# A decoder layer on one core: the last attention round's gate passes laid over slots 9 to 23, and the loads of finished outputs moved three slots later

## The chip, the cores and the metric

The kernel is one program on one core of a Trainium2 chip. Its time is device microseconds (us) of one execution, and the median over runs counts. The engines run side by side and meet at semaphores: TensorE (PE) multiplies, VectorE (DVE), ScalarE (ACT) and GpSimd (POOL) work elementwise, SyncE (SP) issues weight transfers, and ACT's queue issues all other transfers.

## What is computed

One layer of a decoder over 1024 tokens of width 1024, in float32, cut here to what matters:

```
n = rmsnorm(h); proj = n @ w_in         # q, k, v of mixers A and B, gates A and B
o_a = dilated_attention(qa, ka, va)     # 8 heads of 64, softmax under three patterns
o_b = stick_breaking(qb, kb, vb)        # 8 heads of 64, strictly causal
mixed = sigmoid(gate_a) * (o_a @ w_up_a) + sigmoid(gate_b) * (o_b @ w_up_b)
h = h + mixed @ w_out
h = h + memory_attention(rmsnorm(h), rmsnorm(mem))
h = h + swiglu(rmsnorm(h))
return rmsnorm(h)
```

## The kernel before

Everything lies transposed, features on the 128 partitions and the 1024 tokens along the row, in 8 tiles. Precision is kept by splitting each operand into a high and a low part. A product of a weight tile with the 8 operand tiles is therefore three **passes** (high by high, high by low, low by high) of 8 matmuls of 512 columns for each half of the tokens, six passes for a tile. POOL splits each weight tile (`w_hi`, `w_lo`), two buffers deep.

Attention runs in four rounds, one pair of heads of A and one of B each. Three rounds use the plan `ROUND` in a loop, the fourth uses `LAST`, written out. A round is 28 **slots**. There are 24 chunks of up to 512 keys, A's in slots 0 to 11, B's in slots 12 to 23. In slot s PE does, in this order: `logits(s)` (L496), `attend(s - 4)` (L533), `transposes(s - 3)` (L510), and then the **fill** of that slot, passes of the projection tiles (L387). The fill keeps PE at work while the other engines handle a chunk: ACT scales and takes exponentials, DVE runs the cumulative sums of B (`remaining`, L1307 and L1310), and the transposed weights are split into `pt` by ACT (L910) and DVE (L1340), on which `attend` of the next slot waits. DVE reads a finished half of a tile out of its bank (`read_out`, L1217) at the start of the slot behind the one that ended it. ACT stores a gate tile (L942) two slots behind its end.

`LAST` has seven tiles: KB, QB, VB, which feed B, and G0 to G3, gate tiles that nothing in the round reads. Slots 24 to 27 have no logits; they drain the pipeline. `attend(23)`, in slot 27, ends PE's work of the round.

Finished attention outputs go to memory (`store_o`, L965) and come back as the operand of the gated products. `LOAD_O` says in which slots ACT issues the loads of operand tiles 0 to 6 (L952), two in a slot, beginning two slots behind the last fill slot. `ROUND_O` says in which slots ACT already makes the high part of a loaded tile (`round_o`, L958), one in a slot; DVE makes the low part a slot later (`o_rest`, L1260). Tile 7 can be loaded only when the last store has landed (L987, L988). ACT then issues the first four loads of gates (L981), and rounds the tiles that `ROUND_O` left out. The gated product of a weight tile has four units of 12 matmuls each: two with operand tiles 0 to 3, which wait for four low parts, and two with tiles 4 to 7, which wait for all eight. After that PE works without a pause until the output projection.

Of the kernel before, what the change touches and what calls it, by code (L numbers as in the profile page):

```python
# [90 lines left out]
class Plan:  # L91
# [8 lines left out]
    def __init__(self, names, passes, transposes):  # L100
# [40 lines left out]
        for work in self.after["dve"]:  # L141
# [4 lines left out]
ROUND = Plan(("KB", "QB", "QA", "KA", "VB", "VA", "G0", "G1", "G2", "G3"),  # L146
             [3] * 6 + [2] * 6 + [3, 2, 3, 2, 3, 2, 2, 3, 2] + [1] * 6 + [2], {"TB": (12, 14), "TA": (18, 20)})
LAST = Plan(("KB", "QB", "VB", "G0", "G1", "G2", "G3"),
            [2] * 21 + [0] * 7, {"TB": (10, 12)})

LOAD_O = {max(LAST.end.values()) + 2 + n: [k for k in (2 * n, 2 * n + 1) if k < KT - 1] for n in range(4)}
ROUND_O = {min(LOAD_O) + 3 + k: k for k in range(4)}

RAW = {"QA": 0, "KA": 1, "VA": 2, "KB": 0, "QB": 1, "VB": 2, "G0": 0, "G1": 1, "G2": 0, "G3": 1}
SPLIT_NUMBER = {"KB": 3, "QB": 4, "QA": 5, "KA": 6, "TB": 3, "TA": 5}
# [8 lines left out]
def build(nc, xT, memT, positions, gains, weights, ident_d, rope_d, bias_d, mask_d, outT):  # L166
    with ExitStack() as ctx:
# [596 lines left out]
        def _(act):  # L764
# [96 lines left out]
            def round_(i, plan):  # L861
# [41 lines left out]
                for s in range(SLOTS + 2):  # L903
# [43 lines left out]
                    if plan is LAST and s in LOAD_O:  # L947
# [3 lines left out]
                        for k in LOAD_O[s]:  # L951
                            act.dma_start(n_lo[:, k, :].bitcast(F32), o_d[k]).then_inc(tile_in[k], 16)  # L952
                    if plan is LAST and s in ROUND_O:
                        round_o(ROUND_O[s])

            def round_o(k):
                act.wait_ge(tile_in[k], 32)
                act.activation(n_hi[:, k, :], n_lo[:, k, :].bitcast(F32), ACT.Copy).then_inc(o_hi_s, 1)  # L958
# [20 lines left out]
            def load_gates(j, b):  # L979
                for g, at in ((g_a, 0), (g_b, KT)):  # L980
                    act.dma_start(g[:, b, :], gates_d[bass.ds(j + at, 1), :, :].rearrange("o p n -> p (o n)")  # L981
                                  ).then_inc(g_in[b], 16)
# [7 lines left out]
            load_gates(1, 1)  # L990
            for k in range(len(ROUND_O), KT):
                round_o(k)
# [127 lines left out]
        def _(dve):  # L1120
# [99 lines left out]
            def lo_part(name, number, filled):  # L1220
                dst, hi = qk[name[1]][1 if name[0] == "Q" else 3], qk[name[1]][0 if name[0] == "Q" else 2]
                dve.wait_ge(bank_free, filled)
                dve.wait_ge(qk_hi_s, number)
                dve.tensor_tensor(dst[:], raw[:, RAW[name], :], hi[:].bitcast(F32), ALU.subtract).then_inc(qk_lo_s, 1)
# [32 lines left out]
            def o_rest(k):  # L1257

                dve.wait_ge(o_hi_s, k + 1)
                dve.tensor_tensor(n_lo[:, k, :], n_lo[:, k, :].bitcast(F32), n_hi[:, k, :].bitcast(F32),  # L1260
                                  ALU.subtract).then_inc(o_lo_s, 1)

            def round_(i, plan, links):
# [57 lines left out]
                for s in range(SLOTS + 2):  # L1321
# [35 lines left out]
                    for what, name, *rest in plan.after["dve"][s]:  # L1357
# [3 lines left out]
                        elif what == "lo":  # L1361
                            lo_part(name, i * 4 + SPLIT_NUMBER[name], bank + (unit + 2))
                    if plan is LAST and s - 1 in ROUND_O:
                        o_rest(ROUND_O[s - 1])
                assert local[0] == links
# [8 lines left out]

            for k in range(SLOTS + 1 - min(ROUND_O), KT):
                o_rest(k)
# [268 lines left out]
```

## Time and profile before

| what | value |
|---|---|
| median of 3 runs | 1899.01 us (1897.57 to 1899.85) |
| profiled execution, its own time | 1899.36 us |
| its span, first to last instruction | 1897.6 us |
| PE busy | 1782.4 us, 94% |
| DVE busy | 994.6 us, 52% |
| ACT busy | 629.1 us, 33% |
| POOL busy | 709.6 us, 37% |
| mean granted TensorE clock | 0.975 |

The profiled execution's own time is 1.8 us above its span; this lies before the first and after the last instruction. Times in rows are us from the span's start. The round `LAST` lies from 652.5 (its first logits) to 811.2 (end of its last `attend`), and the gated products begin at 817.2. A clock of 1.00 is the higher of TensorE's two levels, 0.50 the lower.

### The profile page before, as it was taken

What the parts mean: (1) busy time and instruction counts of PE and PEld (TensorE: products, weight loads), DVE (VectorE), ACT (ScalarE), POOL (GpSimd) and SP (SyncE); (2) the same over time, 40 slices, a digit from 0 to 9 for tenths busy, and PEclk for the clock granted to TensorE, in tenths of its full rate; (3) what the DMA queues carried; (4) which work ended last, traced back from release to release, by engine and by line L of the source; (5) the groups of instructions that cost most, each with busy time, mean ns of one, the idle gap of its engine ahead of it and who ended that gap; (6) DMA issues with size and microseconds to landing.
All of it is one profiled execution on the core that took longest, in us unless ns stands there. A gap on an engine that the chain in (4) does not pass through costs nothing.

```text
span 1897.6 us, 24569 instructions
## 1 busy us (share of the span) xinstructions
PE 1782.4 (94%) x8610; PEld 1446.1 (76%) x8610; DVE 994.6 (52%) x1490; ACT 629.1 (33%) x1009; POOL 709.6 (37%) x848
## 2 busy tenths in 40 slices
PE   3799999999999999789999899999999999999996
PEld 3677777777778777668887777888888888888884
DVE  7446894688469757865434553332332333333236
ACT  4215773576367557743113332000000000000003
POOL 5632223132313122134553034444434434443435
PEclk8899999999999999889999999999999999999998
DMA  5311112112111211263212011111111111111112
GB/s 191 123 46 46 31 51 64 46 39 66 49 46 38 77 40 50 90 221 133 78 55 78 12 34 45 52 48 44 44 55 44 45 55 44 44 49 50 44 44 89
DMA packets 42201, 118.59 MB, mean 62 GB/s; under 512 B 5136, under 2 KB 13584, under 8 KB 42000
## 3 DMA queue, kind: packets, MB, share of 16 engines
q1 hardware_dynamic: 21312, 75.66, 11.8%
q10 hardware_dynamic: 20816, 41.95, 6.7%
q8 instruction: 46, 0.75, 0.2%
q14 instruction: 27, 0.22, 0.0%
HBM read 97.67 MB, written 18.87 MB: 61 GB/s over the span
## 4 chain that ended last, share of the span: by engine, by line
PE 83%; DVE 7%; ACT 3%; issue 3%; DVEq 0%; ACTq 0%; POOL 0%; DMA 0%; POOLq 0%
PE ps L387 70%; PE ps L533 4%; PE ps L496 3%; PE ps L510 3%; DVE e_row L1310 1%; DVE e_row L1307 1%; DVE pt L1340 1%; DVE h L1550 1%; DVE rows L1319 1%; ACT n_hi L1028 1%; PE ps L529 1%; DVE rms L1421 1%; DVE h L1410 0%; ACT p_m L1054 0%; PE ps L663 0%
## 5 line engine op out<-in xcount | busy, mean ns | idle before, releaser
L350 POOL TENSOR_SCALAR w_hi<-w_stage 128x512 fp32r<-128x512 f32 x276 | 200.9, 745 | 1159.3 <-issue 622.5
L355 POOL TENSOR_TENSOR w_lo<-w_stage,w_hi 128x256 fp32r<-128x256 f32 x552 | 487.4, 913 | 11.5
L387 PE MATMUL ps<-n_hi,w_hi 128*128 128x512 f32 x1536 | 395.2, 398 | 11.0 <-DVE n_lo L1260 7.0
L387 PE MATMUL ps<-n_lo,w_hi 128*128 128x512 f32 x1536 | 386.2, 392 | 0.0
L387 PE MATMUL ps<-n_hi,w_lo 128*128 128x512 f32 x1536 | 385.7, 391 | 0.0
L387 PEld LDWEIGHTS ps<-n_hi,w_hi 128*128 128x128 f32 x1536 | 288.1, 190 | 74.0 <-issue 12.0
L387 PEld LDWEIGHTS ps<-n_lo,w_hi 128*128 128x128 f32 x1536 | 287.3, 188 | 59.8 <-issue 0.2
L387 PEld LDWEIGHTS ps<-n_hi,w_lo 128*128 128x128 f32 x1536 | 286.0, 188 | 58.6
L1410 DVE TENSOR_TENSOR h<-ps,h 128x512 f32<-128x512 f32 (+1 forms) x192 | 132.1, 691 | 160.0 <-PE ps L387 160.0
L1083 ACT ACTIVATE a_hi<-u_f 128x1024 fp32r<-128x1024 f32 x22 | 23.4, 1065 | 466.3 <-DVE u_f L1516 466.3
L1508 DVE TENSOR_TENSOR u_f<-ps,rms 128x512 f32<-128x512 f32 x44 | 30.4, 692 | 205.3 <-PE ps L387 205.3
L910 ACT ACTIVATE pt<-ps 128x256 fp32r<-128x256 f32 (+3 forms) x96 | 77.9, 811 | 134.0 <-PE ps L510 133.9
L1340 DVE TENSOR_TENSOR pt<-ps,pt 128x256 fp32r<-128x256 f32 (+3 forms) x96 | 91.9, 957 | 49.7 <-ACT pt L910 45.6
L387 PE MATMUL ps<-a_hi,w_hi 128*128 128x512 f32 x352 | 111.3, 395 | 1.7 <-DVE a_lo L1518 1.7
L387 PE MATMUL ps<-a_hi,w_lo 128*128 128x512 f32 x352 | 111.7, 396 | 0.0
L387 PE MATMUL ps<-a_lo,w_hi 128*128 128x512 f32 x352 | 111.5, 396 | 0.0
L1217 DVE TENSOR_TENSOR raw<-ps,rms 128x512 f32<-128x512 f32 x80 | 54.8, 685 | 92.5 <-PE ps L387 92.5
L1508 DVE TENSOR_TENSOR g_f<-ps,rms 128x512 f32<-128x512 f32 x44 | 30.3, 691 | 123.1 <-PE ps L387 120.9
L1081 ACT ACTIVATE g_f<-g_f 128x1024 f32<-128x1024 f32 x22 | 23.3, 1061 | 177.8 <-DVE g_f L1508 177.7
L510 PE MATMUL ps<-ident,rows 128*128 128x128 f32 x576 | 81.4, 279 | 0.0
L387 PEld LDWEIGHTS ps<-a_hi,w_hi 128*128 128x128 f32 x352 | 66.1, 188 | 18.8 <-DVE a_lo L1518 2.1
L387 PEld LDWEIGHTS ps<-a_hi,w_lo 128*128 128x128 f32 x352 | 66.1, 188 | 16.2
(175 smaller groups left out, 2212.2 us busy)
## 6 DMA issues: line engine op xcount, KB each, us to landing
w_stage<-weights_in SPq DMA_DIRECT2D x138, 512.0 KB, 3.3
gates_scratch<-raw ACTq DMA_DIRECT2D x16, 512.0 KB, 2.8
o_scratch<-o_sum ACTq DMA_DIRECT2D x64, 64.0 KB, 2.1
n_lo<-o_scratch ACTq DMA_DIRECT2D x8, 512.0 KB, 3.8
g_a<-gates_scratch ACTq DMA_DIRECT2D x8, 512.0 KB, 3.7
g_b<-gates_scratch ACTq DMA_DIRECT2D x8, 512.0 KB, 4.5
h<-x_t_in ACTq DMA_DIRECT2D x8, 512.0 KB, 7.5
out_t<-h ACTq DMA_DIRECT2D x16, 256.0 KB, 2.1
```

Of the source, the lines that this page charges most:

```text
L350: ins = pool.tensor_scalar(w_hi[:, b, at], stage[:, b, at], 1.0, 1.0, ALU.mult, ALU.mult)
L355: ins = pool.tensor_tensor(w_lo[:, b, at], stage[:, b, at], w_hi[:, b, at].bitcast(F32), ALU.subtract)
L387: ins = pe.matmul(bank, w[:, b, c:c + P], mv(k), start=(first and n == 0), stop=(last and n == total - 1))
L496: ins = pe.matmul(ps[:, 2 + h, 0:width(s)], a[hs, blk(qb)], b[hs, at], start=(n == 0), stop=(n == 2 and not diagonal))
L510: ins = pe.transpose(ps_t[:, h, n, :], rows[:, s % 4, h, blk(n)], ident[:])
L533: ins = pe.matmul(ps[:, r, blk(h, 2 * P)], v_of[m][:, c + kb, h, :, :].rearrange("p a d -> p (a d)"), pt[:, h, kb, :, :].rearrange("p a q ...
L910: act.activation(pt[:, :, 0:n, 0, :], ps_t[:, :, 0:n, :], ACT.Copy).then_inc(pt_hi_s, 1)
L1083: act.activation(a_hi[:, f, :], u_f[:, f, :], ACT.Copy).then_inc(a_hi_s, 1)
L1217: dve.tensor_tensor(raw[:, RAW[name], blk(half, HALF)], ps[:, half, :], rms[:, blk(half, HALF)], ALU.mult).then_inc(bank_free, 1)
L1340: dve.tensor_tensor(pt[:, :, 0:n, 1, :], ps_t[:, :, 0:n, :], pt[:, :, 0:n, 0, :].bitcast(F32), ALU.subtract).then_inc(pt_lo_s, 1)
L1410: dve.tensor_tensor(hj, ps[:, bank + half, :], hj, ALU.add).then_inc(bank_free, 1)
L1508: dve.tensor_tensor(dst[:, blk(half, HALF)], ps[:, bank + half, :], rms[:, blk(half, HALF)], ALU.mult).then_inc(bank_free, 1)
```

## The change

Two of the plan's lists change. The 18 passes of KB, QB and VB in slots 0 to 8 stay as they are. The 24 gate passes lay two to a slot in slots 9 to 20; now slots 10, 13, 15, 18, 20 and 22 have one and slots 9, 11, 12, 14, 16, 17, 19, 21 and 23 have two. Since the last fill slot is 23 and no longer 20, `LOAD_O` begins in slot 25 and no longer in slot 22 (25, 26, 27 with two loads, 28 with one). `ROUND_O` is cut to two entries, in slots 28 and 29, where it had four, in slots 25 to 28. The tiles 2 and 3 thus join the tiles 4 to 7 behind the round.

```
 LAST = Plan(("KB", "QB", "VB", "G0", "G1", "G2", "G3"),
-            [2] * 21 + [0] * 7, {"TB": (10, 12)})
+            [2] * 9 + [2, 1, 2, 2, 1, 2, 1, 2, 2, 1, 2, 1, 2, 1, 2] + [0] * 4, {"TB": (10, 12)})
...
 LOAD_O = {max(LAST.end.values()) + 2 + n: [k for k in (2 * n, 2 * n + 1) if k < KT - 1] for n in range(4)}
-ROUND_O = {min(LOAD_O) + 3 + k: k for k in range(4)}
+ROUND_O = {min(LOAD_O) + 3 + k: k for k in range(2)}
```

The reads and stores follow the passes. Reads of gate halves were in slots 11, 12, 14, 15, 17, 18, 20 and 21, and are now in slots 11, 13, 15, 17, 18, 20, 22 and 24. Stores were in slots 13, 16, 19 and 22, and are now in slots 14, 18, 21 and 25.

## Rows read from the trace of the kernel before

**Rows 1.** Busy time and granted clock, by stretch of the round's end.

```profile
core 0: us, PE busy (x) PEld busy (x) DVE busy (x) ACT busy (x) POOL busy (x), PEclk, DMA share, GB/s
...
731.30:792.50 61.20, 53.11 (x318) 42.42 (x316) 58.80 (x68) 50.27 (x64) 13.14 (x12) 1.00 0.15 49
792.50:811.20 18.70, 10.65 (x48) 9.21 (x48) 11.95 (x22) 9.87 (x19) 0.00 (x0) 0.61 0.68 236
811.20:825.80 14.60, 7.59 (x27) 5.60 (x26) 12.06 (x12) 10.07 (x11) 7.58 (x6) 0.68 0.69 244
```

**Rows 2.** Timeline of PE, slot 10's fill and the logits behind it.

```profile
710.56 1.98 PE L387 MATMUL ps<-n_hi,w_hi 128*128 128x512 f32 x8
712.47 0.96 PE L496 MATMUL ps<-qk 64*128 64x512 f32 x6
```

**Rows 3.** Timeline of ACT, slots 11 and 12.

```profile
716.79 0.72 ACT L873 ACTIVATE rows<-rows,stat 128x512 f32<-128x512 f32 x1 [0.30 <-DVE stat L1291]
...
720.19 1.02 ACT L887 ACTIVATE rows<-ps 128x1024 f32<-128x1024 f32 x1 [0.46 <-PE ps L500]
722.07 1.02 ACT L910 ACTIVATE pt<-ps 128x1024 fp32r<-128x1024 f32 x1 [0.85 <-PE ps L510]
```

**Rows 4.** Timeline of DVE, its stretch without pauses and the two pauses in it.

```profile
731.34 1.23 DVE L1307 SCALAR_TENSOR_TENSOR e_row<-rows,e_row 128x1024 f32<-128x1024 f32 x1 [2.44 <-ACT e_row L897]
...
738.24 0.68 DVE L1217 TENSOR_TENSOR raw<-ps,rms 128x512 f32<-128x512 f32 x1
...
764.92 1.23 DVE L1307 SCALAR_TENSOR_TENSOR e_row<-rows,e_row 128x1024 f32<-128x1024 f32 x1 [0.72 <-ACT e_row L897]
...
777.19 1.23 DVE L1307 SCALAR_TENSOR_TENSOR e_row<-rows,e_row 128x1024 f32<-128x1024 f32 x1 [0.65 <-ACT e_row L897]
```

**Rows 5.** Timeline of ACT, slot 22: the step that takes `logits(22)`.

```profile
788.84 0.60 ACT L887 ACTIVATE rows<-ps 128x512 f32<-128x512 f32 x1
```

**Rows 6.** Timeline of PE: a slot's attend and transposes at the higher clock.

```profile
743.86 1.22 PE L533 MATMUL ps<-pt,vA 128*128 128x256 f32 x8 [0.50 <-DVE pt L1340]
744.92 1.03 PE L510 MATMUL ps<-ident,rows 128*128 128x128 f32 x8
```

**Rows 7.** Timeline of PE, slots 23 to 27 and the first gated products.

```profile
793.80 2.07 PE L533 MATMUL ps<-pt,vB 128*128 128x256 f32 x8 [3.39 <-DVE pt L1340]
795.67 1.91 PE L510 MATMUL ps<-ident,rows 128*128 128x128 f32 x8
800.02 2.08 PE L533 MATMUL ps<-pt,vB 128*128 128x256 f32 x8 [2.44 <-DVE pt L1340]
801.90 1.48 PE L510 MATMUL ps<-ident,rows 128*128 128x128 f32 x6
...
808.17 1.22 PE L533 MATMUL ps<-pt,vB 128*128 128x256 f32 x4 [1.41 <-DVE pt L1340]
...
810.75 0.79 PE L533 MATMUL ps<-pt,vB 128*128 128x256 f32 x2 [0.93 <-DVE pt L1340]
817.20 2.07 PE L387 MATMUL ps<-n_hi,w_hi 128*128 128x512 f32 x4 [5.65 <-DVE n_lo L1260]
...
825.77 1.19 PE L387 MATMUL ps<-n_hi,w_hi 128*128 128x512 f32 x4 [1.36 <-DVE n_lo L1260]
```

**Rows 8.** Chain that ended last, from the last store to the last low part.

```profile
813.49 2.10 DMA o_scratch<-o_sum
...
818.28 1.06 ACT n_hi L958
819.37 2.90 DVE n_lo L1260 x2
```

**Rows 9.** ACT's queue: one slot's issues of transfers.

```profile
793.14 0.64 ACTq L965 DMA_DIRECT2D o_scratch<-o_sum  x1
793.90 1.03 ACTq L952 DMA_DIRECT2D n_lo<-o_scratch  x2
```

**Rows 10.** Granted clock around the first gated products (columns as in rows 1).

```profile
820.00:821.00 1.00, 1.00 (x5) 0.81 (x4) 1.00 (x2) 1.00 (x2) 1.00 (x1) 0.80 0.81 315
```

## The prediction

> **What bounds the kernel now.** I read the page first: PE is busy for 94% of the span, so a change of order pays only where PE stands idle or runs at the lower clock. Next came the windows over the last attention round. From 731.3 to 792.5 it has 8.1 us of idle time in 61.2, and DVE is busy for 58.8 of these [rows 1]: DVE paces slots 13 to 22. From 792.5 to 811.2 PE works 10.65 of 18.7 us, at a mean clock of 0.61, and no engine is near full [rows 1]: each slot of the drain is a chain attend, transposes, ACT `pt`, DVE `pt`. From 811.2 to 825.8 PE waits for the operand tiles of the gated products. From 825.77 on, where all eight low parts are there, PE has no idle time to the output projection at 997. So the whole change is worth what it does to the start of the third gated unit, now at 825.77 [rows 7]. That start is my measure. I call the start of `attend(23)` Z, and the end of DVE's `pt` step before it differs from it by 0.04 us. Z is at 810.75, and the third unit starts at Z + 15.0.
>
> **Part 1, five passes taken out of slots 10 to 20.** A pass costs 1.9 us: the second of slot 10 begins at 710.56 and the logits behind it at 712.47 [rows 2]. Slot 10 has one fewer, and PE has no pause there, so `logits(11)` and `logits(12)` come 1.9 us sooner. The other engines do not follow in full. ACT's exponentials of slot 11 wait for DVE's maxima at 716.79 [rows 3], which stand behind DVE's and ACT's own work of slot 10, not behind PE. They fill ACT up to 719.7. The `scaled(12)` step waited 0.46 us for PE and can gain only that. Behind it, `pt` of slot 12 waited 0.85 us more for the transposes, so it moves by at most 0.46 + 0.85 = 1.3 us, and with small gaps I take 1.4. The softmax normalisation, the three softplus steps and with them DVE's first `remaining` (731.34, after 2.44 us of idle time [rows 4]) follow by these **-1.4**. The bounds are 0 and -1.9.
>
> From there DVE paces. Slots 13, 15, 18 and 20 have one pass fewer, but PE's passes there are hidden behind DVE, which has only two pauses, 0.72 and 0.65 us [rows 4]. The first ends with softplus(17), whose logits stand behind slot 16, which keeps two passes; it stays. The second stands behind slots 17 and 18, of which 18 loses a pass: it gives about **-0.35** until DVE's own work is the limit. Bounds 0 and -1.4.
>
> What DVE itself has to do changes by one read. In slots 14 to 22 there were six reads of gate halves and are now five. The one of slot 14 (738.24, 0.6 us from start to start of the next) goes to slot 13, into the pause of 2.44 us before `remaining` [rows 4]: **-0.6**. The one of slot 21 goes to slot 22, and that cancels. The last one goes to slot 24, where DVE waits for the transposes anyway. So `attend(19)`, now at 793.80, moves by -1.4 - 0.35 - 0.6 = -2.35, to 791.45.
>
> **Part 2, five passes added in slots 21 to 23.** In slot 21 two passes (3.8 us) come behind the transposes. They fill the time in which PE waited for `attend(18)` and delay `logits(22)`, but ACT took these logits only at 788.84, right behind its own work [rows 5], so nothing waits. Slot 22's pass lies in the 3.39 us before `attend(19)` [rows 7]. In slot 23 the two passes stand between `transposes(20)` and `attend(20)`. PE waited 2.44 us there. The passes take 3.7, so 1.3 us is not covered.
>
> They also change the clock. Now the clock has fallen by `attend(19)`, since PE did little in slots 22 and 23 before it. `attend(19)` and `transposes(20)` take 3.8 us, where the same pair at the higher clock takes 1.9 [rows 6]. With PE at work through slots 21 to 23 I take the higher clock up to `transposes(21)`. Then from `attend(19)` to `attend(20)` it is 1.9 + 3.75 = 5.65 where it was 6.22: **-0.57**. `attend(20)` and `transposes(21)` take 1.8 for 3.37: **-1.56**. Of the rest, some at the lower clock now (1.22 us for the four matmuls at 808.17 [rows 7]), I take **-0.3**; bounds +1.0 and -0.6, since slots 25 to 27 stay sparse. Sum: Z moves by -2.35 - 0.57 - 1.56 - 0.3 = **-4.8**, to 805.95. At the lower clock throughout, the second part is worth about 0 and Z moves by -2.4.
>
> **Part 3, loads and roundings later.** ACT's queue needs 0.64 us for a store and 1.03 for two loads [rows 9]. In slot 25 these and the gate store are 2.0 us between two `pt` steps that lie some 2.5 apart, so they are just covered. In slot 27 they lie between `o_low(23)` and the last store. Now that store goes out at 813.49 [rows 8], Z + 2.75, held up by a low part that DVE makes before `o_sum(23)`. After the change it follows the loads of slot 27, at Z + 2.6. No difference. It lands after 2.1 us, and the load of tile 7 and four loads of gates take 2.6 us more on the queue. At Z + 7.4 ACT can round again, as now (Z + 7.5, 818.28 [rows 8]). But now it begins with tile 4, and will begin with tile 2. PE's start needs tiles 2 and 3: two roundings of 1.0, and a low part of 1.2, so it comes at Z + 7.4 + 2.0 + 1.2 = Z + 10.6 instead of Z + 6.45. The two units before the third, at the lower clock first, took 7.2 us. The third unit then starts at Z + 17.8, not Z + 15.0: **+2.8**. If the units ran at the higher clock, the last low part would decide, at about Z + 16.9: **+1.9**. Above, the stretch at the lower clock could be twice as long: it ended 3.2 us behind PE's start [rows 7, 10]; under the sparse work of slots 23 and 24 it held from 793.8 to 803.4 [rows 7]. A second such stretch costs 1.7 us more: **+4.5**. I take +2.8.
>
> **Sum.** -4.8 + 2.8 = -2.0 us. The profiled execution took 1899.36, 0.35 above the median of the runs, and 1.8 of it lies outside its span. Neither changes, so the forecast is 1899.0 - 2.0 = **1897.0 us**. The bounds of the terms: with -6.0 for Z and +1.9 it is -4.1; with -2.4 and +4.5 it is +2.1.
>
> **Other work that moves.** POOL's splits of tiles G3 and of the first gated weight move from 746 and 766 to about 753 and 777, still inside DVE's stretch: the same number of collisions. DVE's reads of gates find their banks full, the closest in slot 20 by about 0.1 us by my slot sums. The gates, loaded at the same distance behind Z, are needed only when four units are done.
>
> **Rivals.** *Clock and roundings take it back* (slower). PE is idle for 10 us before the gated products, not 5.65, and the drain is sparse. If the clock falls again before `attend(20)`, Z gains only 2.9 us (the -2.35 and the -0.57), and if the two first gated units run low for longer, +2.8 + 1.7 = 4.5 stands against it: +1.6, 1900.6 us. It decides when the clock is low for more than 5 us behind PE's start. For it: the clock now falls twice between 792 and 811 and is at 0.5 at 817. Against: the passes fill exactly the time in which it fell. The Trainium skill ("TensorE: Matmul & The Clock Gate", section "What's actually happening") says that the low clock is the default and that only activity releases it. The rows agree for the falls seen; the rule speaks for this rival at the gated products, and against it in slots 22 to 24. By it alone the result would lie between this rival and the forecast.
>
> *PE paces more than I think* (faster). If DVE's stretch shrinks by both pauses and slot 10's pass counts in full, `attend(19)` moves by -1.9 - 1.4 - 0.6 = -3.9 and Z by -6.3, and the third unit by -3.5 to -4.4: about 1895.1 us. For it: PE is busy for 53.1 us of the same 61.2 and decides when softplus can begin in the slots behind the pauses. Against: DVE was busy for 96% of the stretch [rows 1, 4].
>
> *Nothing moves* (no change): the start of the chain in slot 12 is held by ACT after all, -1.4 falls away, and the drain gains just what the two roundings cost: -0.6 to +0.4, about 1899 us.
>
> **Chances.** Forecast 0.45, nothing moves 0.23, faster rival 0.15, slower rival 0.17. 0.2% is 3.8 us, and this is about what a measurement of this kernel can tell from no change. Only the faster rival reaches past it, in about half of its cases, and the slower one needs more than its price. Faster 0.11, same 0.82, slower 0.07. The range takes the faster rival's centre and most of the slower one's: 1894.8 to 1900.6.
>
> **What would show it.** In the trace of the changed kernel: DVE's first `remaining` some 1.4 us earlier; `attend(19)` at about 791.5; clock 1.00 up to 798; Z at about 806; PE's first gated product 10.6 us behind Z, the third unit 17.8 behind it. The forecast is wrong if the clock is low in slot 24, if DVE has new pauses between 729 and 790, if the queue's issues in slots 25 to 27 stretch the drain, or if something behind 825.8, which I took as moved in one piece, does not move with it.

## The result, and the profile after

The changed kernel takes 1906.85 us (median of 6, 1902.65 to 1909.55) where before takes 1899.03 (median of 6). The ratio is 1.0039, with a 95% interval of 1.0026 to 1.0052: slower, by 7.8 us by the medians and by about 7.4 by the ratio. Forecast were 1897.0 and a range up to 1900.6. The profiled execution took 1906.71, its span is 1904.9.

The timeline of PE in the changed kernel, around slot 14 (behind slot 13, which lost a pass) and in slot 19:

```profile
730.39 0.80 PE L496 MATMUL ps<-qk 64*128 64x384 f32 x6 [1.28 <-ACT rows L887]
...
734.62 0.77 PE L529 MATMUL ps<-pt,zero_r 128*128 128x512 f32 x1 [3.07 <-issue]
735.18 1.91 PE L533 MATMUL ps<-pt,vA 128*128 128x256 f32 x8
736.89 1.91 PE L510 MATMUL ps<-ident,rows 128*128 128x128 f32 x8
738.45 2.31 PE L387 MATMUL ps<-n_hi,w_lo 128*128 128x512 f32 x8
...
769.04 1.59 PE L533 MATMUL ps<-pt,vB 128*128 128x256 f32 x8 [1.60 <-DVE pt L1340]
...
771.14 2.98 PE L387 MATMUL ps<-n_lo,w_hi 128*128 128x512 f32 x8
```

The eight transposes take 1.91 us, not the 1.03 of [rows 6]; a pass takes 2.98, not 1.9. The clock fell here. In the kernel before it did not, though PE stood for 2.69 us in one pause of slot 14:

```profile
736.51 0.47 PE L529 MATMUL ps<-pt,zero_r 128*128 128x512 f32 x1 [2.69 <-issue]
...
737.77 1.04 PE L510 MATMUL ps<-ident,rows 128*128 128x128 f32 x8
```

PE of the changed kernel at the end of the round:

```profile
795.23 1.22 PE L533 MATMUL ps<-pt,vB 128*128 128x256 f32 x8 [2.17 <-DVE pt L1340]
796.29 1.04 PE L510 MATMUL ps<-ident,rows 128*128 128x128 f32 x8
...
800.84 1.12 PE L533 MATMUL ps<-pt,vB 128*128 128x256 f32 x8
801.79 0.82 PE L510 MATMUL ps<-ident,rows 128*128 128x128 f32 x6
804.57 0.98 PE L533 MATMUL ps<-pt,vB 128*128 128x256 f32 x6 [1.96 <-DVE pt L1340]
...
809.99 0.80 PE L533 MATMUL ps<-pt,vB 128*128 128x256 f32 x2 [0.93 <-DVE pt L1340]
825.19 2.07 PE L387 MATMUL ps<-n_hi,w_hi 128*128 128x512 f32 x4 [14.41 <-DVE n_lo L1260]
```

These answer to [rows 7]. `attend(19)` comes at 795.23, later by 1.4 us and not earlier by 2.35. Z is at 809.99 (810.75 before). PE then stands idle for 14.41 us where it stood for 5.65. The third gated unit starts at 833.52, 7.75 behind the 825.77 of before, and this is the whole difference of the spans (7.3), give or take 0.5.

What fills the 15 us behind Z is shown by the chain that ended last:

```profile
806.42 2.66 DMA o_scratch<-o_sum
809.08 0.01 issue
809.09 0.01 ACT pt L910
809.10 3.97 DMA o_scratch<-o_sum
...
813.16 0.42 DVE o_sum L1353
813.59 0.02 issue
813.61 3.31 DMA o_scratch<-o_sum
816.92 2.00 issue
818.92 0.33 ACTq L988
```

Before, one landing of a store stood in this chain, the last, with 2.10 us [rows 8]. Now there are three, with 2.66, 3.97 and 3.31. The 2.00 us behind the last, in which the chain names nothing, belong to this store too. The 3.31 us end where ACT's roundings of tiles 0 and 1 end (816.92), and not where the store lands. The view of L965 in the window 813.6:813.7 gives the store's own landing, 5.2 us from its issue:

```profile
L965 ACTq DMA_DIRECT2D o_scratch<-o_sum x1: 617/617/617, 813.6 to 813.6; - x1
DMA to landing us min/median/max: 5.2/5.2/5.2
```

That is 818.8, and tile 7's load follows at 818.92. For the last store of before the same view has 2.1. `o_sum` for the last chunk waits too, for the store that empties its buffer. The stretches of the changed kernel (the columns of [rows 1]):

```profile
729.45:795.18 65.73, 55.45 (x311) 44.66 (x311) 59.78 (x69) 51.16 (x65) 15.56 (x12) 0.92 0.14 47
...
810.00:825.20 15.20, 0.79 (x3) 0.50 (x3) 6.64 (x9) 6.18 (x7) 0.00 (x0) 0.50 0.93 348
825.20:833.50 8.30, 8.30 (x24) 6.65 (x25) 5.72 (x5) 5.29 (x6) 6.70 (x6) 0.65 1.01 405
```

The last column but one says that the DMA engines were busy for 93% of the wait, moving 348 GB/s. From DVE's first `remaining` to the end of its step for `attend(19)` there are 65.73 us; DVE works for 59.78 of them. The same stretch of before:

```profile
731.34:793.75 62.41, 53.07 (x318) 42.38 (x316) 60.03 (x70) 51.08 (x64) 13.14 (x12) 0.99 0.15 49
```

DVE's idle time in it grew from 2.4 to 5.95 us.

### The profile page after: what moved, and what is told of

It is laid out like the page before. It is cut to its first block, busy times and chain, and to the rows that moved or that the text cites. A ratio compares the mean times of both kernels' runs of the same rounds, so it can differ in the third digit from the quotient of the medians.

```text
span 1904.9 us, 24569 instructions
## 1 busy us (share of the span) xinstructions
PE 1782.1 (94%) x8610; PEld 1446.0 (76%) x8610; DVE 994.1 (52%) x1490; ACT 628.6 (33%) x1009; POOL 712.2 (37%) x848
## 4 chain that ended last, share of the span: by engine, by line
PE 81%; DVE 7%; ACT 4%; issue 3%; DMA 1%; DVEq 0%; ACTq 0%; POOL 0%; POOLq 0%
PE ps L387 70%; PE ps L533 3%; PE ps L496 3%; PE ps L510 3%; DVE e_row L1310 1%; DVE e_row L1307 1%; DVE h L1550 1%; DVE pt L1340 1%; DVE rows L1319 1%; ACT n_hi L1028 1%; DMA o_scratch<-o_sum 1%; PE ps L529 1%; DVE rms L1421 1%; DVE h L1410 0%; ACT p_m L1054 0%
## 5 line engine op out<-in xcount | busy, mean ns | idle before, releaser
L387 PE MATMUL ps<-n_hi,w_hi 128*128 128x512 f32 x1536 | 395.4, 398 | 18.5 <-DVE n_lo L1260 14.4
L496 PE MATMUL ps<-qk 64*128 64x512 f32 (+3 forms) x576 | 77.8, 376 | 1.3 <-ACT rows L887 1.3
```

The lines of the kernel that those rows point to most:

```text
L387: ins = pe.matmul(bank, w[:, b, c:c + P], mv(k), start=(first and n == 0), stop=(last and n == total - 1))
L496: ins = pe.matmul(ps[:, 2 + h, 0:width(s)], a[hs, blk(qb)], b[hs, at], start=(n == 0), stop=(n == 2 and not diagonal))
```

## The experiments

Each ran beside the kernel before on one chip; e1 to e4 shared a chip, so did e5 to e8 and e9 to e12. The medians of before were 1898.53, 1899.40 and 1898.77, and a difference across these groups is taken between the distances to them. The profiled executions differ by up to 5 us before the round begins, so positions are compared as distances from the round's first logits (652.55 before, 652.59 after). "Third unit" is the start of the third gated unit. The table's positions are those of one profiled execution each; that of e8 took 1891.20, 4.9 below its median, the others lie within 2.3 of theirs.

| run | ratio to before (95%) | attend(19) | Z | store issued to tile 7's load | third unit |
|---|---|---|---|---|---|
| before | 1 | 141.25 | 158.20 | 2.16 | 173.22 |
| after | 1.0039 (1.0026 to 1.0052) | 142.64 | 157.40 | 5.31 | 180.93 |
| e1, loads late | 1.0033 (1.0020 to 1.0045) | 141.23 | 158.15 | 5.56 | 180.60 |
| e2, one slot earlier | 1.0030 (1.0021 to 1.0040) | 142.50 | 159.30 | 4.02 | 180.88 |
| e3, two loads behind store | 1.0032 (1.0020 to 1.0045) | 142.29 | 157.03 | 2.74 | 177.64 |
| e4, other spread | 1.0043 (1.0026 to 1.0059) | 142.84 | 157.83 | 5.91 | 181.02 |
| e5, after, small loads | 1.0006 (0.9997 to 1.0015) | 142.37 | 159.19 | 2.19 | 177.82 |
| e6, before, small loads | 0.9995 (0.9986 to 1.0004) | 141.28 | 158.24 | 2.16 | 173.08 |
| e7, loads late, small | 1.0016 (1.0007 to 1.0025) | 141.23 | 158.17 | 2.19 | 177.16 |
| e8, before, clock kept | 0.9983 (0.9974 to 0.9992) | 141.27 | 156.09 | 2.17 | 170.80 |
| e9, after, clock kept | 1.0022 (1.0012 to 1.0033) | 140.41 | 155.15 | 5.71 | 178.23 |
| e10, as e8, more | 0.9982 (0.9973 to 0.9990) | 141.21 | 154.33 | 2.17 | 169.06 |
| e11, one pass moved | 0.9971 (0.9960 to 0.9982) | 140.06 | 153.55 | 2.17 | 169.70 |
| e12, two roundings | 1.0021 (1.0013 to 1.0030) | 141.28 | 158.60 | 2.17 | 177.65 |

**e1, the loads alone.**

```
 # passes of before
-LOAD_O = {max(LAST.end.values()) + 2 + n: ...
-ROUND_O = {min(LOAD_O) + 3 + k: k for k in range(4)}
+LOAD_O = {max(LAST.end.values()) + 5 + n: ...
+ROUND_O = {min(LOAD_O) + 3 + k: k for k in range(2)}
```

> The passes of before with the later loads and the two roundings of after. Theory L (small stores of attention outputs land late because the 512 KB loads of slots 25 to 28 are in flight with them): the drain's attends stand where they stood before (the last at 810.8), the stores of its last slots take 3 to 5 us to land instead of 2.1, the first gated product starts some 15 us behind the last attend (6.5 before), and the time is 7 to 9 us above before. Rival R (only the two roundings that moved behind the last landing cost, and the rest of the loss comes from the moved passes): 3 to 4 us above before, stores landing in 2.1 us.

Measured: 6.2 us above before (1904.69 against 1898.53), Z where it was, the first product 14.5 us behind it, the third unit 7.4 later. The time lies between the two expectations, and its interval (3.8 to 8.5 us) touches both. Nearly the whole loss is here without any moved pass. In the chain of this run:

```profile
808.49 2.51 DMA o_scratch<-o_sum
...
812.13 3.31 DMA o_scratch<-o_sum
815.44 2.25 issue
817.69 0.33 ACTq L988
```

The view of L965 gives the last three stores 2.7, 4.1 and 5.5 us to their landing (the chain again shows 3.31 of the last). By these landings theory L holds, and rival R, which had them at 2.1, falls.

**e2, loads one slot earlier, three roundings.**

```
 # passes of after
+LOAD_O = {max(LAST.end.values()) + 1 + n: ...
+ROUND_O = {min(LOAD_O) + 3 + k: k for k in range(3)}
```

> The passes of after, loads beginning in slot 24 (one behind the last fill) instead of 25, three roundings in slots 27 to 29. Theory L: the last two stores meet fewer loads and one rounding less stands behind the last landing; the first gated product starts 10 to 12 us behind the last attend (15.2 in after), 3 to 5 us faster than after. Rival R: one rounding, 1 us faster than after.

Measured: the first product 13.55 behind Z, between the two expectations, and a ratio whose interval overlaps that of after. A store landed after 4.91 us, two ahead of the last; the last took 3.9. The loads had met other stores. Its Z is late for another reason: the clock fell in slot 23 (a pass took 3.32 us at 797.93), and from `attend(19)` to Z it is 16.8 us, not the 14.76 of after. This run tells the theories apart only by the landings.

**e3, two loads behind the last store.**

```
 # passes of after
-LOAD_O = {max(LAST.end.values()) + 2 + n: ...
+LOAD_O = {25: [0, 1], 26: [2, 3], 28: [4, 5, 6]}
```

> As after, but tiles 4 and 5 are loaded in slot 28, behind the issue of the last store, instead of in slot 27 ahead of it; roundings as in after. Theory L: the last store lands in about 2.1 to 2.7 us instead of 3.3 to 5.3, and the first gated product starts 2 to 3 us sooner behind the last attend than in after; 2 to 3 us faster than after. Rival R: no change against after.

Measured: in its chain the last store takes 2.67 us, and the first product starts 12.76 us behind Z, 2.4 sooner than in after. That is theory L's number. The times (1904.00; the interval overlaps that of after) can't tell 2.4 us apart from none. In its queue the last two stores are shown as one group:

```profile
811.14 2.89 ACTq L965 DMA_DIRECT2D o_scratch<-o_sum  x2
814.15 1.50 ACTq L952 DMA_DIRECT2D n_lo<-o_scratch  x3
...
816.17 0.33 ACTq L988 DMA_DIRECT2D n_lo<-o_scratch  x1
```

**e5 to e7, the loads' bytes taken away.** One edit, made to after, to before, and to e1. It is on the seven loads of L952; tile 7's load keeps its bytes, though the expectation speaks of eight:

```
-act.dma_start(n_lo[:, k, :].bitcast(F32), o_d[k]).then_inc(tile_in[k], 16)
+act.dma_start(n_lo[:, k, 0:16].bitcast(F32), o_d[k][:, 0:16]).then_inc(tile_in[k], 16)
```

> The kernel after, but the eight loads of finished outputs bring only 16 of 1024 columns each (the operand tiles then hold old values in the rest), so that they hardly use the DMA engines; issues, waits and roundings stay. Theory L (stores queue behind the loads' bytes): stores land in 2.1 us in slots 25 to 28, the first gated product starts 10 to 12 us behind the last attend instead of 15, and the time falls 3 to 5 us below after, to 2 to 4 us above before. Rival Q (the number of issues on ScalarE's queue costs, not their bytes): as after, 7 us above before.

> The kernel before with the same cut of its eight loads to 16 columns; the control for the two others. Theory L: its stores already landed in 2.1 us where they decided, so it gains at most 1 us. If it gains 3 us or more, the loads' bytes also cost before, and the theory explains less of the difference.

> The passes of before with the later loads and two roundings of after, loads cut to 16 columns. Set against e6 it is the price of two roundings and the later issues alone: the forecast's +2.8 (bounds +1.9 and +4.5). Set against e5 it is the price of the moved passes alone: the forecast said -4.8; from the profiles seen so far I now expect -1, between -2 and 0.

Measured: 1900.93, 1898.11 and 1902.48 us. Without the bytes after is 2.8 us above its control, e6, and with them it was 7.8 above before. The first product of e5 comes 11.04 us behind Z, as theory L had it. The control itself gains nothing that can be told. e7's ACT queue issues as many loads at the same places as e1's, and the store is followed by tile 7's load 2.19 us after its issue:

```profile
814.48 0.62 ACTq L965 DMA_DIRECT2D o_scratch<-o_sum  x1
815.21 0.53 ACTq L952 DMA_DIRECT2D n_lo<-o_scratch  x1
...
816.67 0.33 ACTq L988 DMA_DIRECT2D n_lo<-o_scratch  x1
```

So it is the bytes and not the issues; rival Q falls. The DMA engines' share of busy time behind the last attends shows the same. First the window 811 to 814 of e1, then two windows of e7, whose round lies 2.3 us later:

```profile
811.00:814.00 3.00, 0.00 (x0) 0.00 (x0) 0.53 (x2) 0.56 (x1) 0.00 (x0) 0.50 1.03 351
```

```profile
811.00:814.00 3.00, 0.79 (x2) 0.50 (x2) 2.06 (x5) 0.98 (x3) 0.00 (x0) 0.50 0.18 29
814.00:817.00 3.00, 0.00 (x0) 0.00 (x0) 0.12 (x1) 1.21 (x2) 0.00 (x0) 0.50 0.31 50
```

e7 against e6 is the price of two roundings moved behind the landing, with the bytes gone: 4.4 us by the medians, 4.1 by the third unit. e5 against e7 is the price of the moved passes: -1.6 us by the medians, +0.7 in the two profiles. The profile of e5 is one in which the clock fell in slot 23, as in e2: from `attend(19)` to Z it is 16.8 us.

**e12, two roundings alone.**

```
 # before; the low parts behind the round start at len(ROUND_O)
-ROUND_O = {min(LOAD_O) + 3 + k: k for k in range(4)}
+ROUND_O = {min(LOAD_O) + 3 + k: k for k in range(2)}
```

> The kernel before with only the two first roundings inside the round (slots 25 and 26), so that tiles 2 and 3 are rounded behind the last landing as in after; passes and loads stay. The forecast's part 3 alone: first gated product 10.6 us behind the last attend (6.45 before), third unit 17.8 to 19 behind it (15.0), time 2.8 to 4.2 us above before. If the later loads are what costs and not the roundings: within 1 us of before.

Measured: 1902.40 against 1898.77, +3.6 us. The last store lands after 2.11 us, the first product comes 11.05 behind Z, and the third unit 19.05 behind it. Part 3 of the forecast, on its own, was right in kind and, counted from Z to the third unit, 1.2 us too small.

**e4, another spread of the passes.**

```
-[2] * 9 + [2, 1, 2, 2, 1, 2, 1, 2, 2, 1, 2, 1, 2, 1, 2] + [0] * 4
+[2] * 15 + [1] + [2] * 3 + [1] * 5 + [0] * 4
```

> Loads and roundings as in after, but the gate passes lie two to a slot up to slot 18, save slot 15, and one to a slot in 19 to 23: slots 10 and 13 keep two as before. Theory C (a pass taken out of slots 10 and 13 turns into idle time of TensorE around 730, the clock falls there and again at 770, and this eats what the earlier chain had gained): no low clock between 725 and 790, the last attend 2 to 4 us earlier than in after, and the time 2 to 4 us below after. Rival D (VectorE paces slots 13 to 22 whatever the clock): last attend within 1 us of after, time as after.

Measured: the time of after, and the chain of slot 12 where before had it (78.76 us behind the first logits, 78.79 before, 76.86 after). `attend(19)` is as late as in after. The expectation of theory C was missed: the clock fell all the same, at another place. PE, with one pass in slot 15:

```profile
752.01 0.47 PE L529 MATMUL ps<-pt,zero_r 128*128 128x512 f32 x1 [2.16 <-issue]
```

and the windows of the run before and behind that pause:

```profile
750.00:753.00 3.00, 0.99 (x7) 0.98 (x8) 2.93 (x5) 2.91 (x4) 3.00 (x4) 1.00 0.00 0
753.00:757.00 4.00, 4.00 (x18) 3.62 (x17) 3.93 (x5) 1.88 (x3) 0.41 (x1) 0.57 0.38 131
```

PE worked for 1.0 of 3 us, and then the clock was low. It was low again in slot 23 (0.57 from 797 to 801). The run could not tell C from D. A direct test was needed.

**e9, the clock kept in after.** Zero-weight matmuls where PE waits, added onto the bank that is open, so they add zeros:

```
+ZEROS = {14: (0, 11), 17: (0, 6), 19: (1, 6), 23: (1, 8)}   # and (0, 5) at the end of slot 13
+def zeros(half, count):
+    for _ in range(count):
+        pe.matmul(ps[:, half, :], zero_r[:], qkB_k_hi[:, 0:HALF], start=False, stop=False)
```

> The kernel after, with matmuls of zero weights added onto the gate bank that is open at the time, where TensorE waits in the changed plan (5 at the end of slot 13, 11 before the attend of slot 14, 6 in 17, 6 in 19, 8 in 23); they add zeros. Theory C (the pauses that the removed passes leave let the clock fall at 732 and 769, and the slow attends, transposes and passes then make VectorE wait): no low clock between 725 and 790, VectorE idle for 2 to 3 us less in that stretch, attend(19) 140 to 141 us behind the round's first logits instead of 142.4, and the time 1.5 to 3 us below after. Rival P (POOL's splits and VectorE's own work set the stretch): attend(19) stays at 142 to 143 and the time as after.

Measured: 1903.01 us, ratio 1.0022, where after has 1.0039. That is 3.2 us less, but the two intervals overlap, so the gain rests on the trace. The whole stretch ran at the higher clock:

```profile
731.82:795.34 63.52, 59.93 (x347) 47.21 (x345) 59.92 (x69) 51.40 (x65) 15.07 (x12) 1.00 0.16 50
```

It took 63.52 us for the 65.73 of after, with the same work of DVE (59.92 and 59.78), and `attend(19)` came 2.2 us sooner. Theory C holds for after, rival P falls for those 2.2 us. The stores stay late (the last two in its chain land after 3.7 and, by the view of the store's line, 5.7 us), and so does the kernel.

**e8 and e10, the clock kept in before.** The same idea in the drain, into two free banks; before's plan is untouched.

```
+EARLY = {22: 6, 23: 7}                                   # e10 only, ahead of the attend
+LATE = {22: 5, 23: 9, 24: 7, 25: 5, 26: 3, 27: 24}      # e8: 6, 6, 5, 4, 3, 24
+if plan is LAST and s in LATE:
+    pe.wait_ge(bank_free, B_GATED)
+    for n in range(LATE[s]):
+        pe.matmul(ps[:, n % 2, :], zero_r[:], qkB_k_hi[:, 0:HALF], start=True, stop=True)
```

> The kernel before, unchanged in passes and loads, with matmuls of 512 columns on zero weights into two free banks in slots 22 to 27 (6, 6, 5, 4, 3 and 24 of them), where TensorE waits; their results are overwritten. Theory C (the low clock in the drain costs what the forecast said, 2.1 us, and the two gated units 1.7 us): no low clock between 790 and 826, last attend 2 us earlier, the two units in 5.5 us instead of 7.2, and 2 to 4 us faster than before. Rival E (the added matmuls delay attends and the first product by as much): within 1 us of before.

> The kernel before with zero-weight matmuls in slots 22 to 27, now also ahead of the attends of slots 22 and 23 (6 and 7) and more behind the transposes (5, 9, 7, 5, 3 and 24). If the clock stays high through attend(19), another 1.8 us over the first such run: last attend 154.3 us behind the round's first logits (158.2 before, 156.1 there), time 4 to 5 us below before. If the clock falls at 790 all the same, as there: about 3 us below before.

Measured: 1896.12 and 1895.02 us, 3.3 and 3.8 below before, and both intervals end below 1. In e8 the clock still fell at `attend(19)`, and once more at the third unit, whose first matmuls took 1.59 and 1.91 us for 1.07; both were expected not to. In e10 it fell nowhere between 782 and 830, and Z stands 3.9 us earlier than before, as expected; the time, expected 4 to 5 below, is at 3.8. The third unit waits for DVE there, not for PE:

```profile
815.46 1.07 PE L389 MATMUL ps<-n_lo,w_hi 128*128 128x512 f32 x4
816.36 1.07 PE L389 MATMUL ps<-n_hi,w_lo 128*128 128x512 f32 x4
819.99 1.19 PE L389 MATMUL ps<-n_hi,w_hi 128*128 128x512 f32 x4 [2.56 <-DVE n_lo L1270]
```

**e11, one pass moved, loads where they were.**

```
 # e10, without the six matmuls ahead of the attend in slot 22, and
-EARLY = {22: 6, 23: 7}
+EARLY = {23: 7}
-[2] * 21 + [0] * 7
+[2] * 10 + [1] + [2] * 10 + [1] + [0] * 6
-LOAD_O = {max(LAST.end.values()) + 2 + n: ...
+LOAD_O = {max(LAST.end.values()) + 1 + n: ...
```

> As the run before it in this batch, and one gate pass moved from slot 10 to slot 21, with the loads still beginning in slot 22 and four roundings. The part of the forecast that held (the chain of slot 12 starts 1.9 us sooner) without the later loads. If VectorE's chain keeps the 1.9 us to the end: 1.5 to 2 us faster than the run before it. If the new pause lets the clock fall near 732: no faster than it.

Measured: 1894.26 us, ratio 0.9971, the fastest of all. It beats both kernels: before by 0.2 to 0.4%, and after's ratio lies far above its interval. Against e10 the intervals overlap. The chain of slot 12 comes 1.9 us sooner (76.88) and `attend(19)` 1.15 sooner, but the third unit is no earlier. Two things stand in its profile. One is a low stretch, from 735.4 to 738.8, behind a single pause no longer than the 2.69 us of before:

```profile
734.88 0.47 PE L531 MATMUL ps<-pt,zero_r 128*128 128x512 f32 x1 [2.62 <-issue]
...
736.74 1.91 PE L512 MATMUL ps<-ident,rows 128*128 128x128 f32 x8
```

The other is a store that met loads, with the loads in the slots of before: issued at 803.09, it landed after 4.38 us with the DMA engines busy throughout, and DVE's `o_sum` waited 0.8 us for it. That this move alone pays is not shown.

## Why the prediction was wrong

**Part 1.** The start held: DVE's first `remaining` came 1.9 us sooner, forecast 1.4, bound 1.9. What failed is the step "PE's passes there are hidden behind DVE", taken as if taking them out were free. It was known that PE would only wait instead. But a wait of PE is not neutral: with one pass fewer the pauses in slots 13 and 14 grew to 1.28 + 3.07 us, where before had 2.69 and kept its clock, and the clock was low from 732.1 on for 6.8 us and from 769.6 on for 3.4. The slow attends, transposes and passes made ACT and DVE wait. Such falls stand in all four profiles with this spread (after, e2, e3, e5), in both of the other spreads (e4, e11), and in none of those of before's spread up to 786 (before, e1, e6, e7, e8, e10, e12). The length of the pause alone does not decide: e11 fell behind 2.62 us, before kept its clock behind 2.69. `attend(19)` moved by +1.4 where -2.35 was forecast; e9 gives 2.2 of these 3.7 us to the clock. The forecast looked for clock effects only behind slot 21. The Trainium skill ("TensorE: Matmul & The Clock Gate", section "What's actually happening") has idle time bring the default, low clock back. The trace agrees in kind: the granted clock was 1.00 up to 732 and then 0.50, early in the second of the two pauses. The prediction weighed that rule for the drain and should have applied it to each pause that it created.

The other 1.5 us are DVE's, and e9 shows them with the clock kept. Two more steps failed there. The forecast had the bank that is read in slot 20 full "by about 0.1 us"; DVE waits for it, 1.95 us in after and 1.14 in e9:

```profile
775.97 0.69 DVE L1217 TENSOR_TENSOR raw<-ps,rms 128x512 f32<-128x512 f32 x1 [1.95 <-PE ps L387]
```

```profile
775.50 0.69 DVE L1226 TENSOR_TENSOR raw<-ps,rms 128x512 f32<-128x512 f32 x1 [1.14 <-PE ps L388]
```

In all DVE is idle for 3.6 us of e9's stretch, where the forecast comes to 2.0 (2.4 - 0.35). And one read fewer did not take 0.6 us off its work, but 0.1 (e9) to 0.25 (after). POOL's splits now lie at 779 to 787, where DVE's two scans of 512 columns took 3.26 us for the 2.34 of before; so "the same number of collisions" was not the same price. That these collisions are the missing 0.35 to 0.5 us was not tried.

**Part 2.** Right in kind and size: from `attend(19)` to Z it is 14.76 us and was 16.95, -2.2 where -2.4 was forecast. The clock was 1.00 up to 807. Luck had a hand in the size: e3, with the same passes, has 14.7, but in e2 and e5 the clock fell in slot 23 and the way is 16.8, so that nothing is gained. Of the -4.8 for Z, -0.8 was left, and -3.05 with the clock kept (e9).

**Part 3.** Two steps failed. First, "It lands after 2.1 us". That row came from a moment at which the DMA engines were 17% busy (812 to 814 and 814 to 816). In the forecast the loads were counted on ACT's queue, as time to issue them (1.03 us for two, and that held), but not as 512 KB each on the DMA engines. Seven loads that had been spread over slots 22 to 25 now run in slots 25 to 28, exactly with the stores on which `o_sum(23)` and tile 7 wait. From the last store's issue to tile 7's load it is 5.31 us and was 2.16, and the store itself goes out 0.9 later behind Z. e1 against e7 puts the bytes at 3.4 us by the third unit, all of it between the last store's issue and tile 7's load (5.56 and 2.19), and at 3.1 by the medians; after against e5 at 6.3 by the medians, and at 4.9 from Z to the third unit. I take 3 to 6. Second, the two roundings were priced at +2.8 and cost 4.1 (e7 against e6) to 4.4 (e12, by the third unit): the first product came at Z + 11.1, not + 10.6, and the two units took 7.9 to 8.0 us, not 7.2, since the low clock lasted longer. That lay inside the bounds of +1.9 to +4.5.

**The sum.** Third unit: forecast -2.0, measured +7.75. Z accounts for 4.0 of the difference, the way from Z to the first product for 4.6 (Z + 15.2 for Z + 10.6), the two low-clock units for 1.1. The slower rival had the right sign and part of the cause, roundings and a longer low clock behind PE's start (5.6 us, more than its 5), at +1.6; its other half, a fall ahead of `attend(20)`, did not happen in this profile. No rival had the stores, and this is why the range was too low. Everything behind 825.8 moved in one piece to within 0.5 us, as assumed.

## What to carry to other kernels

When loads are moved, ask what small transfer on the critical path will share the DMA engines with them: its landing time has to be read at that load, not at the quiet moment in which it is now. A pass taken out of a slot that another engine paces does not come for free: the new pause can cost TensorE its clock, and zero matmuls in such pauses were worth 3.3 and 3.8 us in the kernel before. In after they gave 2.2 us up to `attend(19)`; their 3.2 us of the whole time do not stand clear of the intervals. And work that can be done before the last landing (two roundings, 1 us each) costs far more than its own length behind it, 4 us.

## What the runs showed of the hardware

A store of 64 KB landed after 2.1 us where the DMA engines were 16 to 28% busy (the last stores of before, e5 to e8 and e10 to e12). It landed after 2.6 to 6.1 us where loads of 512 KB were issued around it on the same engine's queue (the DMA engines were 82% busy or more in the landings that the chains of after, e1 to e4, e9 and e11 show): the last store took 5.2 us in after, 5.5 in e1, 5.7 in e9, 5.8 in e4, 3.9 in e2, and 2.7 in e3, where three loads came behind it and not one. The chain cuts such a landing short where the waiting engine had other work in between. The granted clock was low from 807 to 831 in after, through an idle time of 14.4 us and for 5.6 us of full work behind it; before, 3.2 us of work behind 5.65 idle sufficed. A single pause of 2.69 us left the clock high in before, one of 2.62 let it fall in e11, and executions of one order of work differ (slot 23 in after and e3 against e2 and e5). Keeping TensorE at work on zeros held the higher clock in the stretches where they lay, 731.8 to 795.3 in e9 and 782 to 830 in e10.
